# An attention stage on one core: values projected last, index weights as three products, plain transposes, token-major outputs

## The reference

```python
proj = h @ w_in                                    # q, k, v, qi, ki, wi
q = apply_rope(rmsnorm(q, q_gain), cos, sin)       # k the same
qi = apply_rope(qi, cos, sin)                      # 8 index heads of 64
ki = apply_rope(rmsnorm(ki, None)[:, :, None, :], cos, sin)[:, :, 0, :]
wi = wi.astype(f32) * (IDX_HEADS ** -0.5)          # 8 index weights a token
...
s_idx = jnp.einsum('bqhd,bkd->bqhk', qib, ki) * idx_scale
score = jnp.einsum('bqhk,bqh->bqk', jax.nn.relu(s_idx), wb)
_, sel = lax.top_k(jnp.where(causal, score, -jnp.inf), topk)
logits = jnp.einsum('bqhd,bqkhd->bhqk', qb, kg) * att_scale
p = jax.nn.softmax(jnp.where(valid, logits, -jnp.inf), axis=-1)
out = jnp.einsum('bhqk,bqkhd->bqhd', p, vg)        # then out @ w_o
```

## Time and profile before

| | us |
|---|---|
| median of 3 runs | 3219.6 (3216.91 to 3222.54) |
| the profiled execution, its own time | 3229.3 |
| its span, from the first to the last instruction | 3227.0 |
| mean granted clock | 0.942 |
| PE busy | 2957.6 (92%) |
| DVE busy | 1898.2 (59%) |
| ACT busy | 1398.6 (43%) |
| last projection step to the end of wi | 2554 to 2590 |
| attention, first logits to the start of wo | 2589.6 to 2792.0 |

### The profile page before, as it was taken

One profiled execution on the slowest core, in us unless ns is written; L12 is line 12 of the kernel. 1 busy time (PEld: TensorE's weight loads), 2 busy tenths in 40 slices (PEclk: granted clock), 3 DMA queues, 4 the chain that ended last, 5 costly groups with the idle time before them and its releaser, 6 DMA issues.

```text
span 3227.0 us, 35793 instructions
## 1 busy us (share of the span) xinstructions
PE 2957.6 (92%) x12812; PEld 2275.4 (71%) x12812; DVE 1898.2 (59%) x2283; ACT 1398.6 (43%) x1824; POOL 219.3 (7%) x167
## 2 busy tenths in 40 slices
PE   7999999976899999999975498999989999989998
PEld 2548888755677777777764376888857766668887
DVE  3436744565988888888886834333267367343332
ACT  2423333233677777777755133322233234333221
POOL 1100100005910000000010000000011100000000
PEclk9999989986999999999987699999999858999999
DMA  6911722334899999999984411222212100022221
GB/s 236 329 63 59 293 79 92 107 123 158 311 337 379 362 378 361 379 361 378 361 322 36 85 66 71 99 92 93 104 61 79 66 1 1 27 78 92 105 92 65
DMA packets 90801, 546.92 MB, mean 169 GB/s; under 512 B 9232, under 2 KB 18848, under 8 KB 32384
## 3 DMA queue, kind: packets, MB, share of 16 engines
q1 hardware_dynamic: 79584, 485.65, 40.7%
q0 software_dynamic: 10816, 59.58, 5.4%
q10 hardware_dynamic: 288, 0.15, 0.0%
HBM read 516.51 MB, written 41.42 MB: 173 GB/s over the span
## 4 chain that ended last, share of the span: by engine, by line
PE 72%; DVE 16%; issue 5%; ACT 3%; DMA 3%; POOL 1%; SPq 0%; DVEq 0%; ACTq 0%; POOLq 0%; PEldq 0%
PE bank L328 40%; PE bank L266 6%; PE bank L1115 5%; PE bank L1119 4%; PE bank L1118 4%; DVE expert_low L2156 4%; DMA arena<-in_we_stream 2%; PE bank L1321 1%; PE bank L1341 1%; PE bank L1333 1%; ACT expert_high L1535 1%; PE bank L1308 1%; PE bank L1099 1%; DVE expert_x_low L2241 1%; DVE arena L2258 1%
## 5 line engine op out<-in xcount | busy, mean ns | idle before, releaser
L2156 DVE TENSOR_TENSOR expert_low<-arena,expert_high 128x2048 fp32r<-128x2048 f32 x291 | 683.8, 2380 | 101.3 <-ACT expert_high L1535 83.7
L1535 ACT ACTIVATE expert_high<-arena 128x1024 fp32r<-128x1024 f32 x582 | 596.7, 1057 | 211.7 <-PE bank L1115 120.7
L328 PE MATMUL bank<-high_b,weight_parts 128*128 128x512 f32 x1872 | 594.0, 399 | 34.0 <-DVE low_b L2394 21.6
L694 DVE TENSOR_TENSOR weight_parts<-ring_pages,weight_parts 128x1024 fp32r<-128x1024 f32 x185 | 226.7, 1226 | 562.2 <-ACT weight_parts L686 561.5
L686 ACT ACTIVATE weight_parts<-ring_pages 128x1024 fp32r<-128x1024 f32 x185 | 196.0, 1060 | 597.1 <-PE bank L328 553.0
L328 PEld LDWEIGHTS bank<-high_b,weight_parts 128*128 128x128 f32 x1872 | 353.5, 190 | 125.6 <-issue 36.8
L328 PE MATMUL bank<-low_b,weight_parts 128*128 128x512 f32 x896 | 351.3, 392 | 0.0
L1115 PE MATMUL bank<-expert_high,expert_x_low 128*128 128x512 f32 x768 | 308.9, 402 | 13.7 <-DVE expert_low L2156 10.2
L1118 PE MATMUL bank<-expert_high,expert_x_high 128*128 128x512 f32 x768 | 300.4, 391 | 0.0
L1119 PE MATMUL bank<-expert_low,expert_x_high 128*128 128x512 f32 x768 | 300.1, 391 | 0.0
L328 PE MATMUL bank<-hidden_parts,weight_parts 128*128 128x512 f32 x1056 | 241.5, 391 | 4.3 <-DVE hidden_parts L2440 4.3
(11 more groups left out here) (449 smaller groups left out, 4142.9 us busy)
## 6 DMA issues: line engine op xcount, KB each, us to landing
arena<-in_we_stream SPq DMA_DIRECT2D x294, 1024.0 KB, 6.6
ring_pages<-in_wb_stream SPq DMA_DIRECT2D x93, 1024.0 KB, 4.8
ring_pages<-in_wa_stream SPq DMA_DIRECT2D x49, 1024.0 KB, 4.9
arena<-in_mod POOLq DMA_DIRECT2D x16, 1024.0 KB
xbuf<-arena POOLq DMA_DIRECT2D x25, 512.0 KB, 15.9
arena<-xbuf SPq DMA_DIRECT2D x17, 512.0 KB, 7.3
ybuf<-arena SPq DMA_DIRECT2D x16, 512.0 KB, 2.6
arena<-kd SPq DMA_DIRECT2D x8, 512.0 KB, 21.9
```

What stands on the lines that cost most here:

```text
L328: ins = pe.matmul(o, lhsT, rhs, start=start, stop=stop)
L694: nc.vector.tensor_tensor(low, src, high.bitcast(F32), ALU.subtract).then_inc(weights_split, 1)
L1535: nc.scalar.activation(ehigh[c % HIGH_E][:, at], ring_e[c % RING_E][:, at], ACT.Copy) \
L2156: nc.vector.tensor_tensor(elow[c % RING_E][:], ring_e[c % RING_E], ehigh[c % HIGH_E][:].bitcast(F32), ALU.subtract).then_inc(weights_split ...
```

## The change

The weights of the values (dv) come last in the weight stream, behind the index keys, and their two projections are done in the two steps that finish the norms and rotations. The index weights are made from split parts: the job wip has 8 weight columns stationary and 512 tokens moving, 24 products into one bank, of which ScalarE copies 8 rows; the job wi then turns them in four small transposes. The probabilities are turned by plain transposes against the identity, unscaled. The value product has the probabilities stationary and the 64 value columns moving, so the output has tokens on the partitions; ScalarE scales it by the reciprocal of the row's sum while it reads the bank, two operations a pair of heads in place of one. Eight more transposes for each tile t (mx, 6 steps after its last pair) bring the output back, and its high and low parts are made from the bank. The maximum is taken with its sign turned (the query gain holds the factor), so VectorE's scaling of it and the diagonal fall away.

```diff
@@ the order of jobs
 for _s in range(NR + 2):
     if _s < NR:
         JOBS_B += [f"pr{_s}"]
+    else:
+        JOBS_B += ["wip" if _s == NR else "wi"] + [f"dv{_s - NR}{t}" for t in range(NTX)]
...
-_k = JOBS_B.index(f"pr{2 * KT}")
-JOBS_B[_k:_k] = [f"dv{n}{t}" for n in range(2) for t in range(NTX)]
-JOBS_B += ["wi"]
...
+TURN_LAG, VALUE_LAG, MIX_LAG = 3, 4, 6
+for _s in range(NSTEP):
+    if _s >= AH + MIX_LAG - 1 and (_s - MIX_LAG + 1) % AH == 0:
+        JOBS_B += [f"mx{(_s - MIX_LAG + 1) // AH - 1}{n}" for n in range(2)]
@@ TensorE
+                elif s == NR:
+                    ps = opened("wip")
+                    pe.wait_ge(S["small_operands"], 3)
+                    for kt in range(KT):
+                        for w, h in ((0, low_p), (0, high_b), (1, high_b)):
+                            ins = pe.matmul(ps[0:IH, :], wi_parts[:, w, kt, :], h[:, kt, :],
+                                            start=(kt == 0 and h is low_p), stop=(kt == KT - 1 and w == 1))
+                    ins.then_inc(bank_done, 1)
...
-            for t in range(NTX):
-                for kt in range(KT):
-                    for part in (high_b, low_p):
-                        ins = pe.matmul(ps[:, t * IH:(t + 1) * IH], part[:, kt, t * P:(t + 1) * P].bitcast(F32),
-                                        wiw[:, kt, :], start=(kt == 0 and part is high_b),
-                                        stop=(kt == KT - 1 and part is low_p))
...
-                    pe.wait_ge(S["b_diag_ready"], k + 1)
+                    pe.wait_ge(S["b_exped"], k + 1)
                     ps = opened(f"pt{k}")
                     for b in range(t + 1):
-                        ins = pe.matmul(ps[:, b * P:(b + 1) * P], pp[:, k % 4, b * P:(b + 1) * P],
-                                        diag[:, k % 4, :], start=True, stop=True)
+                        ins = pe.transpose(ps[:, b * P:(b + 1) * P], pp[:, k % 4, b * P:(b + 1) * P], ident[:])
...
-                        ins = pe.matmul(av[r:r + 64, 0:P], vt[:, b, h * HD:(h + 1) * HD],
-                                        pT[:, k % 2, b * P:(b + 1) * P], start=(b == 0), stop=(b == t))
+                        ins = pe.matmul(av[:, c:c + HD], pT[:, k % 2, b * P:(b + 1) * P],
+                                        vt[:, b, h * HD:(h + 1) * HD], start=(b == 0), stop=(b == t))
@@ ScalarE
-                    copied(act, nc.scalar.activation(oT[:, h // 2, t * P:(t + 1) * P], psum[JB[name] % 8][:, 0:P],
-                                                     ACT.Copy), S["b_o_ready"], k // 2 + 1, name)
+                    for n in (k - 1, k):
+                        t, h = PAIRS[n]
+                        ins = nc.scalar.activation(mixed_rows[t % 2][:, h * HD:(h + 1) * HD],
+                                                   psum[JB[name] % 8][:, h % 2 * HD:(h % 2 + 1) * HD], ACT.Copy,
+                                                   scale=rsm[:, n % 8:n % 8 + 1])
@@ VectorE
-                link(nc.vector.reciprocal(rsm[:, b:b + 1], sm[:, b:b + 1]))
-                nc.vector.tensor_scalar(diag[:, b, :], ident[:], rsm[:, b:b + 1], None, ALU.mult) \
-                    .then_inc(S["b_diag_ready"], 1)
+                nc.vector.reciprocal(rsm[:, s % 8:s % 8 + 1], sm[:, b:b + 1]).then_inc(S["b_sums_ready"], 1)
...
-                    nc.vector.tensor_scalar(nmx[:, b:b + 1], mx[:, b:b + 1], -float(HD) ** -0.5, None, ALU.mult) \
-                        .then_inc(S["b_logits"], 1)
```

More of the change, by code:

```diff
@@ L637, in block_kernel @@
         pT = page(36, 2, T)
-        diag = page(37, 4, P)
+        wi_rows = page(36.5, T)
         rope = page(37.5, P)
         half1 = page(37.625, P)
-        oT = page(38, KT, T)
+        mixed_rows = [page(42, D), page(43.5, D)]
         sqt = page(42, 2, T)
@@ L1285, in _ @@
                 if s < NR:
[L1286 to L1289, removed]
                     by_columns(f"pr{s}", (ROPED[s][0], ROPED[s][1]), lambda kt: (high_b[:, kt, :], low_p[:, kt, :]),
                                split_before=None if s else 2 * KT + FFT)
+                elif s == NR:
[6 more added lines that the diff above has]
+                    ins.then_inc(bank_done, 1)
+                else:
+                    ps = opened("wi")
+                    pe.wait_ge(S["small_operands"], 4)
+                    for t in range(NTX):
+                        ins = pe.transpose(ps[:, t * IH:(t + 1) * IH], wi_rows[0:IH, t * P:(t + 1) * P], ident[0:IH, 0:IH])
+                    ins.then_inc(bank_done, 1)
+                if s >= NR:
+                    by_rows([f"dv{s - NR}{t}" for t in range(NTX)], ("dv", s - NR),
+                            lambda kt: (high_b[:, kt, :], low_p[:, kt, :]))
                 if 1 <= s <= NR and ROPED[s - 1][2]:
@@ L1303, in _ @@
                     pe.matmul(ps[:], rope, roped_tile(s - 2), start=True, stop=True).then_inc(bank_done, 1)
-            ps = opened("wi")
-            for t in range(NTX):
-                for kt in range(KT):
-                    for part in (high_b, low_p):
-                        ins = pe.matmul(ps[:, t * IH:(t + 1) * IH], part[:, kt, t * P:(t + 1) * P].bitcast(F32),
-                                        wiw[:, kt, :], start=(kt == 0 and part is high_b),
-                                        stop=(kt == KT - 1 and part is low_p))
[L1311 to L1314, removed]
+            pe.wait_ge(S["b_rotated"], 2 * KT)
+            for s in range(NSTEP):
+                if s >= AH + MIX_LAG - 1 and (s - MIX_LAG + 1) % AH == 0:
+                    t = (s - MIX_LAG + 1) // AH - 1
+                    pe.wait_ge(S["b_o_ready"], AH * (t + 1))
+                    for n in range(2):
+                        ps = opened(f"mx{t}{n}")
+                        for i in range(4):
+                            ins = pe.transpose(ps[:, i * P:(i + 1) * P],
+                                               mixed_rows[t % 2][:, (4 * n + i) * P:(4 * n + i + 1) * P], ident[:])
+                        ins.then_inc(bank_done, 1)
                 if TURN_LAG <= s < NPAIR + TURN_LAG:
@@ L1343, in _ @@
                     if h == 1 and t < NTX - 1:
+                        pe.wait_ge(S["b_rotated"], NR)
                         for i in range(IH):
@@ L1741, in _ @@
                 if s < NR:
-                    weights_high_part(act, ahead("dki", ROPED[s][0], ROPED[s][1]), split_to)
+                    weights_high_part(act, ahead("dv", ROPED[s][0], ROPED[s][1]), split_to)
+                else:
+                    weights_high_part(act, ahead("dv", "dv", s - NR, KT, True), split_to)
             n_relu = 0
-            for s in range(NPAIR + VALUE_LAG):
+            for s in range(NSTEP):
                 if 1 <= s <= NPAIR:
@@ L2453, in _ @@
             dve.wait_ge(S["b_rope_in"], 48)
+            link(nc.vector.tensor_scalar(col("qk_gain", 0), col("qk_gain", 0), -float(HD) ** -0.5, None, ALU.mult))
+            dve.wait_ge(S["small_operands"], 2)
+            nc.vector.tensor_tensor(wi_parts[:, 1], wiw[:], wi_parts[:, 0].bitcast(F32), ALU.subtract) \
+                .then_inc(S["small_operands"], 1)
             for s in range(NR + 2):
-                if s == 2 * KT:
-                    for n in range(2):
-                        weights_low_part(dve, ahead("dki", "dv", n, KT, True), split_to)
+                if s == NR + 1:
+                    ps = result(dve, "wi")
+                    link(nc.vector.tensor_scalar(wi, ps[:, 0:NTX * IH].rearrange("p (t h) -> p t h", h=IH),
+                                                 float(IH) ** -0.5, float(HD) ** -0.5, ALU.mult, ALU.mult))
+                    dve.sem_inc(free("wi"), 1)
+                if s >= NR:
+                    weights_low_part(dve, half_of("dv", s - NR, KT, True) + 1, split_to)
                 if 1 <= s <= NR and ROPED[s - 1][2]:
@@ L2514, in _ @@
             rounds, first = TOPK // 8, 3
-            for s in range(NPAIR + 1):
+            for s in range(NSTEP):
                 if s < NPAIR:
```

108 lines of the change are left out of this document (66 added, 42 removed).

## The result

The changed kernel takes 3212.0 us in the median of 12 runs (3186.0 to 3216.0), the kernel before 3222.5 (3216.9 to 3236.9): a ratio of 0.9932, with 0.9912 to 0.9953 as its interval, 0.7% faster. The median hides the shape: five runs lie at 3186.0 to 3191.2 with a mean granted clock of 0.938 to 0.942, seven at 3211.4 to 3216.0 with 0.930 to 0.933, and none between. The profiled execution is one of the five (3190.6, span 3188.7).

What follows compares the result with a forecast made beforehand. TensorE was taken as the bound, 72% of the chain, with VectorE bounding t = 2. Projections -22.7 and attention +37.4 us gave +14.7: 3244 for the profiled execution, 3234 for the median, slower than 3219.6; range 3195 to 3244.

Steps and rivals of the forecast that it cites:

- the case forecast: Attention: the clock falls at head 7 of t = 2 and stays low to the end; 3226 to 3243, chance 0.46.
- the rival's 3200 to 3213: Attention: the clock recovers at head 5 of t = 3, where mx and turn transposes stand in a row; chance 0.30.
- Up to the attention: Projections: index weights -21.1, norm stall -4.4, possible weight stall +0.3, last rotation +2.5; sum -22.7 us.
- the stall for the norm: End of the projections: TensorE's 4.4 us wait for the index keys' norm goes, as the values now lie over it.
- the last rotation: Before the attention: tile 0's index products wait for it, with nothing to cover GpSimd's 1.28 us and two VectorE additions; +2.5.
- the stall on weights: Values' projection: VectorE splits later weight halves behind the norm's reciprocal; risk 0 to +3.8 us, taken as +0.3.
- The step at the low level: Attention at the low clock: turn, values and logits together 1.95, 3.03, 4.11, 5.19 us for t = 0 to 3.
- Which clock each tile has: Attention: low in t = 1, falling at head 7 of t = 2, then low to the end; attention +37 us.
- The argument against it: Against recovery at head 5 of t = 3: 22 transposes had run at the earlier rise, here 12 stand between matmuls.
- The fall in t = 2: Clock falls at head 7, a pair with two selection rounds: TensorE's about 2.1 us waits for VectorE's 3.8.
- The smaller steps: Attention: full-level step of t = 3 2.78 us where 3.16 was; VectorE's one-round pair in t = 2 2.3 us.

Runs made afterwards that it cites:

- run 2: Changed kernel with the eight mx transposes of tile t = 2 moved from head 5 of t = 3 to the end; 3214.1 us.
- run 1: Kernel before with only the change's projection part (values last, index weights as three products, small transposes), attention untouched; 3200.9 us against 3224.8.
- run 3: Changed kernel with each of the eight mx transposes of t = 2 made three times over; 3193.7 us.
- run 4: Changed kernel with 102 more transposes in the turns of t = 2, nine a pair at nine heads and three elsewhere; 3173.1 us.
- run 7: Changed kernel with value products 128 columns wide and a lighter filling of repeated transposes in t = 1 and t = 2; 3177.2 us.
- run 11: Changed kernel with the turn made as real fp32 matmuls and value products 128 columns wide; 3185.6 us.
- runs 5: Changed kernel with the turn's plain transposes made as real fp32 matmuls against the identity; 3201.4 us.
- run 6: Changed kernel with value products 128 columns wide instead of 64, both heads' values for each head's probabilities; 3189.2 us.
- run 12: Changed kernel with one selection round instead of two at heads 7, 11 and 15 of t = 2; 3185.7 to 3193.4 (six runs), 3211.2 to 3222.1 us (four).

## Why the prediction was wrong

The forecast was 3234, slower; the kernel is 0.7% faster. That 3212.0 lies in the range of 3195 to 3244 is luck: none of the twelve runs lies in the 3226 to 3243 of the case forecast, and none in the rival's 3200 to 3213 but two at its upper edge, which by their clock belong to the other case. The upper group (3214.3 in its median) is 20 under the 3234 of its case, the lower one (3189.2) 18 under the 3207 of its own. By its own steps, from the profiles of before, of the changed kernel (lower group) and of run 2 (which stands for the upper one), first logits of a tile to first logits of the next:

| us | before | predicted | run 2 | changed, profiled |
|---|---|---|---|---|
| t = 0 | 35.4 | -1.8 | 30.8 (-4.6) | 30.8 (-4.6) |
| t = 1 | 54.4 | -3.3 | 45.4 (-9.0) | 46.1 (-8.3) |
| t = 2 | 50.9 | +7.4 | 58.6 (+7.7) | 59.7 (+8.8) |
| t = 3 to the start of wo | 61.6 | +35.1 | 84.3 (+22.7) | 57.4 (-4.2) |
| attention | 202.4 | +37.4 | +16.7 | -8.4 |

**Up to the attention: right.** -22.7 was forecast, and run 1 has -23.9 with an interval of -20 to -28. Each term is in the rows: 5.56 for 5.5, 0.34 for 0.5, the stall for the norm gone, 1.27 + 0.70 behind the last rotation for +2.5, and the stall on weights as it was before (3.7). That the profiled execution begins its attention 29.0 earlier may be in part the execution shown of before, 6.8 over its median. The values take 21.79 + 22.00 = 43.8 us, which is 192 x 0.229 and not the 48 of the prediction; nothing hangs on it.

**The step at the low level: mis-sized, and enough to turn the sign.** The prediction put "turn 0.22(t+1) + 0.29, values and logits 0.43(t+1) + 0.29 each". The price of each matmul was right; the 0.29 beside a group was read from the logits and put on all three. Values took 0.40 less than that, turns 0.10 less, so that a step is 0.50 to 0.55 shorter. The earlier trace rows could have warned: the old values were 0.62 and 1.05 there, which is 0.43(t+1) + 0.19. With the measured steps in the prediction's own count (16, 16, 8 and 16 pairs) its sum loses 29.5 us and goes from +14.7 to -14.8. An execution that is low to the end, as the prediction told it, costs the attention +16.7 and not +37.4. That is run 2: 3214.1, ratio 0.9962 (0.9950 to 0.9975), faster than before and not slower. Run 2 keeps all the work of the change, so nothing else is needed for the sign. That its t = 2 comes out near the forecast (+7.7 for +7.4) is luck: a pair costs 3.57 and not 4.11, but more pairs than the last eight were at 0.50, as in 2650 to 2660 of the changed kernel.

**Which clock each tile has: half wrong.** "I expect it to stay low through t = 2 and ... to the end" was the case in seven of the twelve runs, as their mean clock says, which is that of run 2; none of the seven was profiled. In the profiled one, and by their clock in the four beside it, the level came back at the mx of head 5, the rival to which 0.30 was given; run 2 (never) and run 3 (always) show that these transposes decide between the groups, which lie 25 us apart, as the rival's -27 said. The argument against it, 12 transposes between matmuls instead of 22 in a row, wasn't a reason to go by. What tips one execution of the same kernel to either side was not tried apart.

**The fall in t = 2: near the place, wrong cause.** I put it to the pair with two rounds, at head 7. The level does fall when TensorE has done the logits of head 7, behind the window that ends at 2666, and beside a wait:

```profile
2667.01 1.54 PE L1348 MATMUL bank<-arena 128*128 128x64 f32 x6 [1.66 <-ACT arena L1781]
```

But VectorE is still at head 6 then. Its two rounds of head 7 begin behind the fall:

```profile
2668.49 0.68 DVE L2589 MAX8 m<-arena 128x8 f32<-128x512 f32 x1
...
2669.99 0.69 DVE L2589 MAX8 m<-arena 128x8 f32<-128x512 f32 x1
```

What made TensorE wait is in the chain. At head 5 VectorE makes the low parts of the finished tile's output (L2539), so the maximum of head 6 (L2573) comes late, and with it ScalarE's exponential and the copy of the turned probabilities behind it (L1781):

```profile
2662.02 0.70 DVE low_p L2539
...
2662.93 0.70 DVE low_p L2539
...
2665.28 0.56 DVE arena L2573
...
2666.59 0.38 ACT arena L1781
```

From the start of the first low part to VectorE's next round (2663.76) are 1.74 us, and the wait is 1.66. The prediction counts mx as transposes only and has no term for this work of VectorE, in a tile of which it says that VectorE is the bound.

Whether the wait brings the level down isn't settled: no run moves the low parts alone. More of the same transposes keep the level (run 4), but they also shorten this wait: the longest from head 5 of t = 2 on is 0.43 us there. The length of a wait doesn't decide alone: run 7 kept 1.00 over waits of 1.60, 1.23 and 1.05 us in t = 2, and run 11 lost it beside one of 1.22 in t = 2 and kept it over one of 1.47 in t = 3. A turn of matmuls or wide values alone left some 50 us low in their profiles (runs 5 and 6); both together brought the level back before t = 3 (run 11). That fits with the amount of TensorE's work in a step having a part; with one profile of each kernel it shows no more.

One reading of the rows was wrong too: "t = 1 began low and stayed low, without a pause of TensorE". Between the windows of the earlier trace rows the kernel before was at 1.00 for the last index products of t = 1 and the pairs behind them, and lost it 1 us after a wait of 1.92:

```profile
2630.00:2636.00 6.00, 4.08 (x22) 2.50 (x20) 4.81 (x9) 4.48 (x11) 0.12 (x1) 1.00 0.00 0
```

**The smaller steps.** A step of t = 3 at the full level is 2.48, not 2.78; the 0.2 beside the groups holds for the logits (1.05), less for the turn (0.59) and not for the values (0.84). VectorE's pair with one round is 2.38 us between two MAX8, predicted 2.3:

```profile
2663.76 0.69 DVE L2589 MAX8 m<-arena 128x8 f32<-128x512 f32 x1
...
2666.14 0.68 DVE L2589 MAX8 m<-arena 128x8 f32<-128x512 f32 x1
```

## What to carry to other kernels

A fixed cost beside a group of matmuls belongs to that kind of group: read it from each kind's own rows, and put its two ends through the whole sum, since half a microsecond in each of the 56 steps that were counted at the low level decided the sign here. Where the clock has two levels, making TensorE's step leaner can cost more than it saves: look which level the stretch behind it will have, and where another engine sets the pace, try repeated transposes before giving a lean step up. Before an experiment is taken as a test of a cause, look whether its edit acts ahead of the effect: that of run 12 came behind it. A median over two groups of runs says little; give both groups and look for the place where they part.

## What the runs showed of the hardware

- 102 transposes whose results are thrown away made the changed kernel 16 us faster than its lower group and 41 faster than its upper one (run 4).
- TensorE was busy without a pause for 80 us at 0.50 (run 2), and for 38 us at 1.00 with the same steps and the eight transposes of mx among them (run 4, t = 3). The Trainium skill, "TensorE: Matmul & The Clock Gate", Part 1 (The HAM clock gate), has activity release the throttle; being busy in the profile's sense did not do so in run 2.
- At the full level an fp32 product with 128 stationary columns costs 0.84 / 4 = 0.21 us with 64 columns moving (changed kernel, t = 3) and 0.89 / 4 = 0.22 with 128 (run 6).
- The level rose while only transposes ran: values and logits took 1.60 and 2.00 us ahead of the eight of mx and 0.84 and 1.05 behind them (changed kernel, 2716.11).
